# A two-layer decoder trunk on one core: float32r projections with five products a step in place of six

## The reference

```python
x = x + 0.5 * swiglu(rms_norm(x, g1), w_gate, w_up, w_down)        # hidden width 2816
x = x + mixer(rms_norm(x, g2)) @ w_out      # layer 0: GLA and retention heads; layer 1: S5 groups and windowed attention
x = x + memory_attend(rms_norm(x, g3), mem_k, mem_v)               # 4 heads over 256 memory tokens
x = x + 0.5 * swiglu(rms_norm(x, g4), w_gate, w_up, w_down)
```

## Time and profile before

| | |
|---|---|
| runs | 2966.88 us median of 3 (2958.37 to 2967.17) |
| profiled execution | 2961.86 us, span 2959.7 us, mean granted clock 0.929 |
| TensorE products (PE) | 2675.8 us, 90% of the span, 20495 instructions |
| VectorE (DVE) | 1237.5 us, 42% |
| ScalarE (ACT) | 865.1 us, 29% |
| GpSimd (POOL) | 156.7 us, 5% |
| moved | 258.93 MB, 87 GB/s over the span |

### The profile page before, as it was taken

The page is one execution under the profiler, slowest core; times in us unless marked ns, Lnnn a source line. Parts: engine busy times, 40 slices in busy tenths (PEclk is TensorE's granted clock), DMA queues, the critical chain, the costliest instruction groups (busy, mean ns, idle before and its releaser), DMA issues. The chain is left out here.

```text
span 2959.7 us, 48853 instructions
## 1 busy us (share of the span) xinstructions
PE 2675.8 (90%) x20495; PEld 2552.0 (86%) x20495; DVE 1237.5 (42%) x1634; ACT 865.1 (29%) x1116; POOL 156.7 (5%) x127
## 2 busy tenths in 40 slices
PE   6999999949768988999998999999779898899998
PEld 6999998947668968999998999998548886899998
DVE  6434424342145334433426524434753533443342
ACT  4421213121145324421215412222243522441221
POOL 0000000000000000000007300005000000000000
PEclk9999999965589999999999999999879999999999
DMA  3222222211113542222222222221012553222222
GB/s 114 90 85 79 90 73 79 87 50 29 32 65 121 185 164 69 88 93 79 90 73 85 90 73 93 89 64 62 24 41 80 178 187 101 69 87 89 80 83 89
DMA packets 76360, 258.93 MB, mean 87 GB/s; under 512 B 9780, under 2 KB 19204, under 8 KB 75232
## 3 DMA queue, kind: packets, MB, share of 16 engines
q1 hardware_dynamic: 75728, 255.81, 25.7%
q0 software_dynamic: 528, 1.64, 0.2%
HBM read 246.85 MB, written 10.57 MB: 87 GB/s over the span
## 5 line engine op out<-in xcount | busy, mean ns | idle before, releaser
L96 DVE TENSOR_TENSOR w_low<-w_raw,w_high 128x1024 fp32r<-128x1024 f32 (+2 forms) x360 | 471.7, 1310 | 1272.1 <-ACT w_high L92 1271.7
L340 PE MATMUL ps<-h_high,w_high 128*128 128x272 f32 x4192 | 888.1, 294 | 86.1 <-DVE h_low L283 39.9
L340 PE MATMUL ps<-h_high,w_low 128*128 128x272 f32 x4192 | 880.2, 292 | 0.0
L340 PE MATMUL ps<-h_low,w_high 128*128 128x272 f32 x4192 | 878.0, 292 | 0.0
L92 ACT ACTIVATE w_high<-w_raw 128x1024 fp32r<-128x1024 f32 (+2 forms) x360 | 400.2, 1112 | 1385.7 <-PE ps L340 1277.0
L340 PEld LDWEIGHTS ps<-h_high,w_high 128*128 128x128 f32 x4192 | 674.7, 193 | 92.8 <-DVE h_low L283 41.6
L340 PEld LDWEIGHTS ps<-h_low,w_high 128*128 128x128 f32 x4192 | 673.0, 192 | 0.0
L340 PEld LDWEIGHTS ps<-h_high,w_low 128*128 128x128 f32 x4192 | 668.1, 193 | 0.0
L340 PE MATMUL ps<-ffn_hid,w_high 128*128 128x272 f32 x2816 | 474.5, 291 | 24.6 <-PEq L165 24.6
L340 PEld LDWEIGHTS ps<-ffn_hid,w_high 128*128 128x128 f32 x2816 | 402.6, 191 | 26.1 <-issue 26.1
L340 PE MATMUL ps<-ffn_hid,w_low 128*128 128x272 f32 x1408 | 294.1, 290 | 0.0
(11 more groups left out here) (369 smaller groups left out, 1851.4 us busy)
## 6 DMA issues: line engine op xcount, KB each, us to landing
w_raw<-in_ffn_w_gate SPq DMA_DIRECT2D x88, 512.0 KB, 3.2
w_raw<-in_ffn_w_up SPq DMA_DIRECT2D x88, 512.0 KB, 3.3
w_raw<-in_ffn_w_down SPq DMA_DIRECT2D x64, 704.0 KB, 4.1
mem_ring<-in_cache_mem_k SPq DMA_DIRECT2D x32, 512.0 KB, 7.7
mem_ring<-in_cache_mem_v SPq DMA_DIRECT2D x32, 512.0 KB, 7.5
w_raw<-in_even_w_in SPq DMA_DIRECT2D x26, 512.0 KB, 3.3
w_raw<-in_mem_w_k SPq DMA_DIRECT2D x16, 512.0 KB, 3.3
w_raw<-in_mem_w_v SPq DMA_DIRECT2D x16, 512.0 KB, 3.2
```

Of the source, the lines that this page charges most:

```text
L96: return nc.vector.tensor_tensor(core.low[s][:, 0:kt * P], core.raw[s][:, 0:kt * P], core.high[s][:, 0:kt * P].bitcast(F32), ALU.subtract)
L340: last = nc.tensor.matmul(acc[s][:, a, :], w, x[:, k, a * width:(a + 1) * width], start=(k == 0 and n == 0), stop=(k == kt - 1 and n == 2))
```

## The change

For the up and down projections and the two mixer inputs, the high and the low part of a k tile lie side by side in one row of 1088 columns: high columns 0 to 271, low columns 0 to 89, high columns 272 to 543, low columns 272 to 361, then the remaining 182 + 182 low columns. Against the high weights this is three products, of 362, 362 and 364 columns; against the low weights two products of 272. A tile takes three banks in place of two: in the first two, high and low-weight sums in 272 columns and low-activation sums in 90 beside them; in the third the other 364 low-activation sums. So the sums of the low activations come out apart and are added when the tile is finished: in `"gate"` and `"copy"` ScalarE copies them into the output tile with two instructions and VectorE adds the full sums, then scales in place; in `"add"` VectorE adds them to x with two instructions ahead of the full sums. What writes the split activations writes the new layout, the low part with two instructions in place of one. The loops over pairs of SyncE, ScalarE and VectorE are written out for these projections; TensorE's stays a counted loop. The other projections use the old code, on the same memory seen in the old layout.

```diff
+NEAR = 90
+FAR = TOK // 2 - NEAR
+SPAN = TOK // 2 + NEAR
+
+class Packed:
+    def all(self, k):
+        return self.ap[:, k]
+    def high(self, k):
+        return self.ap[:, k, 0:2 * SPAN].rearrange("p (a c) -> p a c", c=SPAN)[:, :, 0:TOK // 2]
+    def lows(self, k):
+        return (self.ap[:, k, 0:2 * SPAN].rearrange("p (a c) -> p a c", c=SPAN)[:, :, TOK // 2:SPAN],
+                self.ap[:, k, 2 * SPAN:].rearrange("p (a c) -> p a c", c=FAR))
...
+    packed = isinstance(src, Packed)
...
-        acc = [core.ps[:, 2 * s:2 * s + groups, 0:width] for s in range(2)]
-        sums = core.ps[:, 4:4 + groups, 0:width]
+        joined = sem("joined")
+        stride = 3 if packed else 2
+        acc = [core.ps[:, stride * s:stride * s + groups, 0:width] for s in range(2)]
+        sums = core.ps[:, 2 * stride:2 * stride + groups, 0:width]
+        def low_acc(s):
+            return (core.ps[:, 3 * s:3 * s + 2, TOK // 2:SPAN],
+                    core.ps[:, 3 * s + 2, 0:2 * FAR].rearrange("p (a c) -> p a c", c=FAR))
...
-            if side is not None:
+            if side is not None or (packed and eng is not nc.tensor):
...
+                def copy_low(s, i):
+                    if low_copied is None:
+                        return
+                    act.wait_ge(tile_done, i * 2 + s + 1)
+                    if finish == "gate" and i >= 1:
+                        act.wait_ge(product_ready, i)
+                    to = in_groups((sg, up)[s][:] if finish == "gate" else dst[:, 2 * i + s], cols)
+                    near, far = low_acc(s)
+                    nc.scalar.activation(to[:, :, 0:NEAR], near, ACT.Copy)
+                    nc.scalar.activation(to[:, :, NEAR:], far, ACT.Copy).then_inc(low_copied[s], 1)
...
                 def pair(i):
                     split_high(0, i * 16 + (base[0] + 16), i * 2 + 1)
+                    copy_low(0, i)
                     aside("act", act, i * 2 + 1)
                     if finish == "gate":
                         gate(i)
                     split_high(1, i * 16 + (base[1] + 32), i * 2 + 2)
+                    copy_low(1, i)
                     aside("act", act, i * 2 + 2)

                 steps(act, 0, last_pair, pair)
+                copy_low(0, last_pair)
                 if after is not None:
                     split_high(0, base[0] + 16 * pairs, 2 * last_pair + 1, after[1])
...
                     gate(last_pair)
+                copy_low(1, last_pair)
...
+                def together(s, i, out):
+                    dve.wait_ge(low_copied[s], i + 1)
+                    nc.vector.tensor_tensor(out, out, acc[s], ALU.add).then_inc(joined, 1)
+                    dve.wait_ge(joined, i * 2 + s + 1)
+                def finish_packed(s, i):
+                    if finish == "gate":
+                        to = in_groups((sg, up)[s][:], cols)
+                        together(s, i, to)
+                        nc.vector.tensor_tensor(to, to, in_groups(rstd, cols), ALU.mult).then_inc((gate_scaled, up_scaled)[s], 1)
...
+                    if finish == "add":
+                        near, far = low_acc(s)
+                        nc.vector.scalar_tensor_tensor(out[:, :, 0:NEAR], near, scale, out[:, :, 0:NEAR], ALU.mult, ALU.add
+                                                       ).then_inc(joined, 1)
+                        nc.vector.scalar_tensor_tensor(out[:, :, NEAR:], far, scale, out[:, :, NEAR:], ALU.mult, ALU.add
+                                                       ).then_inc(joined, 1)
+                        dve.wait_ge(joined, i * 4 + (2 * s + 2))
+                        ins = nc.vector.scalar_tensor_tensor(out, acc[s], scale, out, ALU.mult, ALU.add)
+                    else:
+                        together(s, i, out)
+                        ins = nc.vector.tensor_tensor(out, out, in_groups(rstd, cols), ALU.mult)
+                    ins.then_inc(psum_free[s], 1)
...
+                            def full():
+                                for b, lo, n in ((0, 0, SPAN), (1, SPAN, SPAN), (2, 2 * SPAN, 2 * FAR)):
+                                    ins = nc.tensor.matmul(core.ps[:, bank + b, 0:n], w_high, x[:, lo:lo + n],
+                                                           start=(k == 0), stop=(k == kt - 1))
+                                return ins
+                            def rest():
+                                for b, lo in ((0, 0), (1, SPAN)):
+                                    nc.tensor.matmul(core.ps[:, bank + b, 0:TOK // 2], w_low, x[:, lo:lo + TOK // 2],
+                                                     start=False, stop=False)
```

More of the change, by code:

```diff
@@ L212, in gate @@
                     nc.scalar.activation(sg[:], sg[:], ACT.Silu).then_inc(gate_ready, 1)
+                def copy_low(s, i):
[8 more added lines that the diff above has]
+                    nc.scalar.activation(to[:, :, NEAR:], far, ACT.Copy).then_inc(low_copied[s], 1)
                 if norm:
                     for k in range(kt):
[L216 removed]
+                        x_out = src.high(k) if packed else src[0][:, k]
+                        x_in = in_groups(x_tiles[k], cols) if packed else x_tiles[k]
+                        nc.scalar.activation(x_out, x_in, ACT.Copy, scale=core.vec(gain + k)).then_inc(x_high, 1)
                         if k == 3:
@@ L282, in _ @@
                         dve.wait_ge(x_high, k + 1)
-                        nc.vector.scalar_tensor_tensor(src[1][:, k], x_tiles[k], core.vec(gain + k),
-                                                       src[0][:, k].bitcast(F32), ALU.mult, ALU.subtract).then_inc(x_ready, 1)
+                        if packed:
+                            near, far = src.lows(k)
+                            x_near, x_far = low_sides(x_tiles[k])
+                            high = src.high(k).bitcast(F32)
+                            nc.vector.scalar_tensor_tensor(near, x_near, core.vec(gain + k), high[:, :, 0:NEAR], ALU.mult,
+                                                           ALU.subtract)
+                            nc.vector.scalar_tensor_tensor(far, x_far, core.vec(gain + k), high[:, :, NEAR:], ALU.mult,
+                                                           ALU.subtract).then_inc(x_ready, 1)
+                        else:
+                            nc.vector.scalar_tensor_tensor(src[1][:, k], x_tiles[k], core.vec(gain + k),
+                                                           src[0][:, k].bitcast(F32), ALU.mult, ALU.subtract).then_inc(x_ready, 1)
                         if k == 4:
@@ L336, in tile @@
                         w_low = core.low[s][:, k * P:(k + 1) * P]
+                        if packed:
+                            x = src.all(k)
+                            bank = 3 * s
+                            def full():
[7 more added lines that the diff above has]
+                                                     start=False, stop=False)
+                            if k == 0:
+                                full()
+                                rest()
+                            else:
+                                rest()
+                                last = full()
+                            continue
                         passes = ((w_high, src[0]), (w_high, src[1]), (w_low, src[0]))
@@ L583, in ffn @@
     with ExitStack() as ctx:
-        hid = [ctx.enter_context(nc.sbuf_tensor(f"{name}_hid{s}", [P, HT, TOK], F32R)) for s in range(2)]
+        hid = Packed(ctx.enter_context(nc.sbuf_tensor(f"{name}_hid", [P, HT, 2 * TOK], F32R)))
         for half in range(2):
@@ L588, in ffn @@
             norm = of_x(core, VEC[f"ffn{which}_norm"] + KT * layer) if half == 0 else None
-            projection(nc, core, f"{name}_up{half}", gate_up, HT, KT, core.h, TOK, "gate", hid, after=(down, HT),
+            projection(nc, core, f"{name}_up{half}", gate_up, HT, KT, core.packed, TOK, "gate", hid, after=(down, HT),
                        norm=norm, scaled=True, beside=beside if half == 0 else None)
@@ L600, in even_mixer @@
         pr = ctx.enter_context(nc.sbuf_tensor("even_proj", [P, EVEN_TILES, TOK], F32))
-        projection(nc, core, "even_in", core.pairs_of(a["even_w_in"]), EVEN_TILES // 2, KT, core.h, TOK, "copy", pr,
+        projection(nc, core, "even_in", core.pairs_of(a["even_w_in"]), EVEN_TILES // 2, KT, core.packed, TOK, "copy", pr,
                    after=after_in, norm=of_x(core, VEC["mix_norm"]), scaled=True)
@@ L2187, in odd_mixer @@
             b = s5_buffers(nc, core, held)
-            projection(nc, core, "odd_in", core.pairs_of(a["odd_w_in"]), ODD_TILES // 2, KT, core.h, TOK, "copy", pr,
+            projection(nc, core, "odd_in", core.pairs_of(a["odd_w_in"]), ODD_TILES // 2, KT, core.packed, TOK, "copy", pr,
                        after=(glu, 4), norm=of_x(core, VEC["mix_norm"] + KT), scaled=True,
@@ L2209, in build @@
         core.x = sb("x", [P, KT, TOK])
```

(4 more changed lines are left out.)

27 lines of the change are left out of this document (added).

## The result

The kernel after takes 3011.18 us (median of 4, 3006.99 to 3016.27), before 2967.03, 44 us less. The ratio on record is 1.0163 (1.0135 to 1.0191): 48 us slower (40 to 57). The profiled execution took 3009.42 us around a span of 3007.6, 47.9 more than the span of before.

The account below looks back on a forecast made before the run. TensorE, busy 90% of the span, was taken as the bound. Terms -26.9 + 12.6 + 6.6 + 3.0 + 5.4 + 4.8 = +5.5 us gave 2972 us against the median, 0.2% up; range 2960 to 2997.

Parts of the forecast that it names:

- the first term: Inside the projections' loops, one product fewer a step saves 11.8 ns over 2280 steps: 26.9 us gained.
- the gain of nothing: Lower bound of the gain inside the loops: if all product time goes by the column, dropping a product saves nothing.
- Rival A: Product time goes by the column, 0.460 ns each, 166.5 ns for 362 columns; slower, 2999 us; chance 22%.
- Up to down: Eight seams from up to down projection: copies, added sum and split low part cost 1.58 us each, 12.6 us lost.
- Down to up: After a down projection, three accumulations replace one: 0.83 us at each of eight seams, 6.6 us lost.
- The clock: After up to down, all eight stretches fall to the lower clock, three more than before: 4.8 us lost.
- The norm starts: TensorE's third tile at six starts: 0.48 us later at four (table loads gone), 1.76 at two; 5.4 us lost.
- The two mixer inputs: Their ends gain copies and an add, 3.0 us lost together; their norm starts cost 1.76 us each.
- work given to them there costs nothing: Inside a projection's loop ScalarE and VectorE have time to spare, so added work is free there.
- rival C: Seams dearer: slower copies, adds at upper bounds, table loads staying, two clock levels; some 12 us more, 2984; chance 12%.

Follow-up runs that it names:

- the 512-column stream: The kernel before with an added end block where TensorE alone streams 48 products of 512 columns, other engines silent: 226.7 ns a product.
- no_low_sums: The kernel after without adding the low sums at the end of a tile, TensorE's products kept: 2974.5 us, ratio 1.0037 to the kernel before.

## Why the prediction was wrong

The step that failed is the first term: "I take 11.8 ns a product, independent of width", 26.9 us gained. Measured: the three wide products left 15.6, 19.6 and 15.4 ns, 15 more than three times 11.8, which is more than the 11.8 of the dropped product. The step went from 751.6 to 754.5, 6.6 us lost over 2280 steps: 33.5 us from the forecast, and below the gain of nothing that I had set as the lower bound. The two widths I took the slope from, 256 and 272, are both multiples of 16; the new ones are not. With 80 low columns, multiples of 16 throughout, the same change gives back 21 us and a step of 743: there the dropped product is worth some 8 ns, not at the widths of the change. Multiples of 16 are not all of it, for 112 and 48 have them too and step at 747.3 and 748.1; what makes a product of a given width and place cost what it does stays open. Rival A's 166.5 ns for 362 columns was hit by chance: its mechanism is excluded by the 512-column stream.

Up to down was right: 3.37 to 5.02 us from product to product, 1.65 for 1.58. Down to up was right: 1.37 to 2.24, 0.87 for 0.83. no_low_sums prices both, with mixer ends, norm starts and clock, at 37.

The clock was right in kind and somewhat low in size: I foresaw three more dips of 1.6 us, 4.8. In the eight windows after up to down TensorE did 170 products, where a stretch at the full level did 34: 102 missing, of 0.151 us each, are 15.4 us. Before there were four dips of 1.6 and one of 2.75 (49 products against 27), 9.2. So 6 us went there, less than the deeper dips suggest, since part of the low level falls into the standing (TensorE is busy for 5.1 of the 6.0 us). The one dip after a down projection, for which I counted nothing, cost another 1.5.

The norm starts were right where the loads went: in the after trace no line of the weight split loads a table, and the wait right before the third tile fell in three of four FFNs. But the second tile starts 1 us later, as the low parts had it, and the third came 1.4, 1.2, 0.5 and 1.4 us later from the start of the norm, for 0.48 foretold. The two mixer inputs came out 4.7 and 6.0 us longer, with their pace, for 3.3 each.

Missing altogether was GpSimd: "work given to them there costs nothing" holds only while VectorE keeps its own pace; beside GpSimd it had no slack left, 6 to 7 us. Stages that the change doesn't touch were some 8 us shorter in this one profile, mostly in time at the lower clock; that is not of the change.

Together: from the +5.5 us of the forecast to the +47.9 between the two spans lead 33.5 of the pace, 6 to 7 of GpSimd, 3 of the clock, 3 of the norm starts, 1 of the seams and -8 elsewhere; some 3 us are not placed. One sum in the prediction is wrong too: the parts of rival C as it names them (copies 2.2, adds 3.0, loads 5.2, clock 7.2 us) make nearer 18 than 12 us.

## What to carry to other kernels

Before trading many products for fewer wide ones, time TensorE alone at the very widths and starts: here the three wide products cost 15 ns more beside their columns than the rate of the old width promised, and what one product less was worth went into that. What was added at the end of a tile was free in the loop, where VectorE kept its own pace, and dear at a barrier; take the barrier away first. And check who else uses the engine that is said to have slack, stage by stage.

## What the hardware showed that I had not expected

- A product of 128 or 182 columns takes 111.6 to 111.9 ns in a stream of float32r products, the same as one another.
- A float32r product of 256 columns or more leaves 9 to 20 ns beyond its columns, by its width and its place; a bfloat16 product of the same stream 2.5 to 3.7.
- After 4.70 us of standing the granted clock was 0.50 to 0.58 in seven of eight stretches of 6 us, 0.72 in the eighth; after 3.08 us it was 0.51 once, 0.72 four times and 1.00 three times; after 1.91 us 0.72 once and 1.00 three times.
- Most of VectorE's operations on SBUF take two to three times as long beside GpSimd's, 0.72 to 1.69 us, and 0.35 to 1.07 for 180 elements; the one right after a sum out of PSUM only 0.73 to 0.82, and the sum that reads PSUM none.
